# Ten gate and up chunks of layer 0 as seven block products instead of eight, and 30 adaLN units moved from the channel mixer of layer 0 into the token mixer of layer 1

## The reference, cut to what matters

```
for l in range(DEPTH):
    with_ctx = l < DEPTH - 1
    mods = jnp.split(c_act @ w_ada[l] + b_ada[l], 6, axis=-1)          # latent condition
    modc = jnp.split(cc_act @ w_ada[l] + b_ada[l], 6, axis=-1)         # context condition
    h = modulate(layernorm(x), sh1, sc1); y = token_mixers(h, hc, ...)
    x = layernorm(ALPHA * x + g1 * y)
    g, u = jnp.split(modulate(layernorm(x), sh2, sc2) @ w_gu[l], 2)    # 1024 -> 2 x 2816
    x = layernorm(ALPHA * x + g2 * ((silu(g) * u) @ w_down[l]))
```

## Time and profile before

| | us |
|---|---|
| median of 3 runs | 2298.59 (2298.22 to 2300.33) |
| the profiled execution's own time | 2300.03 |
| its span, first to last instruction | 2298.2 |
| PE busy | 2245.5 (98% of the span) |
| DVE / ACT / POOL busy | 1206.5 / 940.1 / 1108.4 |
| chain that ended last | PE 84%, DVE 8%, ACT 4% |

### The profile page before, as it was taken

One profiled execution on the slowest core, in us unless ns is written; L12 is line 12 of the kernel. 1 busy time (PEld: TensorE's weight loads), 2 busy tenths in 40 slices (PEclk: granted clock), 3 DMA queues, 4 the chain that ended last, 5 costly groups with the idle time before them and its releaser, 6 DMA issues.

```text
span 2298.2 us, 34335 instructions
## 1 busy us (share of the span) xinstructions
PE 2245.5 (98%) x12986; PEld 2054.7 (89%) x12986; DVE 1206.5 (52%) x2473; ACT 940.1 (41%) x1874; POOL 1108.4 (48%) x868
## 2 busy tenths in 40 slices
PE   7999999999999999999999999999999999999997
PEld 4899989989999999999998888888888899888887
DVE  6979766538731646654832364656637536112114
ACT  4232466437622751111112364256546547222223
POOL 1334455435534453433534563456545567545545
PEclk9999999999999999999999999999999999999999
DMA  6634300122224445443523453221223256333335
GB/s 270 218 116 133 102 19 28 57 79 82 60 65 149 154 161 183 135 154 111 167 88 118 152 170 123 69 60 38 65 87 97 83 193 189 119 96 101 110 117 186
DMA packets 122535, 270.27 MB, mean 118 GB/s; under 512 B 13972, under 2 KB 14228, under 8 KB 120984
## 3 DMA queue, kind: packets, MB, share of 16 engines
q1 hardware_dynamic: 112032, 242.28, 32.9%
q10 hardware_dynamic: 10360, 26.09, 3.5%
HBM read 254.68 MB, written 10.49 MB: 115 GB/s over the span
## 4 chain that ended last, share of the span: by engine, by line
PE 84%; DVE 8%; ACT 4%; POOL 1%; issue 1%; DMA 1%; ACTq 1%; SPq 0%; DVEq 0%
PE ps L2047 32%; PE ps L2059 13%; PE ps L2049 12%; PE ps L2476 7%; PE ps L2160 7%; PE ps L2429 3%; PE ps L2411 3%; PE ps L2392 2%; PE ps L2236 1%; POOL w_lo L610 1%; DVE pt L1741 1%; DVE max_c L1724 1%; DVE ada_unused_merge_c L1261 1%; DMA raw<-in_stream 1%; ACT p_sb L987 1%
## 5 line engine op out<-in xcount | busy, mean ns | idle before, releaser
L610 POOL TENSOR_TENSOR w_lo<-raw,w_hi 128x512 fp32r<-128x512 f32 x648 | 888.5, 1394 | 915.9 <-ACT w_hi L688 915.1
L688 ACT ACTIVATE w_hi<-raw 128x512 fp32r<-128x512 f32 x648 | 377.4, 627 | 663.7 <-PE ps L2049 215.1
L2047 PE MATMUL ps<-h_hi,w_lo 128*128 128x512 f32 (+1 forms) x832 | 304.7, 366 | 0.0
L2047 PE MATMUL ps<-h_hi,w_hi 128*128 128x512 f32 (+1 forms) x832 | 303.9, 365 | 0.0
L2047 PE MATMUL ps<-h_lo,w_hi 128*128 128x512 f32 (+1 forms) x832 | 303.9, 365 | 0.0
L622 POOL TENSOR_TENSOR p_sb<-p_sb,row_inv 128x768 f32<-128x768 f32 (+1 forms) x160 | 179.1, 1128 | 196.6 <-DVE row_inv L1734 195.2
L1851 DVE TENSOR_TENSOR ps<-silu_g,ps 128x512 f32<-128x512 f32 (+3 forms) x52 | 36.7, 706 | 355.1 <-PE ps L2047 191.1
L2047 PEld LDWEIGHTS ps<-h_hi,w_lo 128*128 128x128 f32 x832 | 156.2, 188 | 18.6 <-POOL w_lo L610 0.3
L2047 PEld LDWEIGHTS ps<-h_lo,w_hi 128*128 128x128 f32 x832 | 156.2, 188 | 18.4
L2047 PEld LDWEIGHTS ps<-h_hi,w_hi 128*128 128x128 f32 x832 | 156.2, 188 | 18.3
L2476 PE MATMUL ps<-h_hi,w_lo 128*128 128x384 f32 (+1 forms) x408 | 146.7, 360 | 1.0 <-ACT gates_a L1024 0.7
(11 more groups left out here) (248 smaller groups left out, 5345.1 us busy)
## 6 DMA issues: line engine op xcount, KB each, us to landing
raw<-in_stream SPq DMA_DIRECT2D x648, 256.0 KB, 3.0
ada_raw_gate_up<-in_w_ada SPq DMA_DIRECT2D x48, 512.0 KB, 3.5
ada_raw_tokens_a<-in_w_ada SPq DMA_DIRECT2D x16, 512.0 KB, 4.7
ada_raw_merge_c<-in_w_ada SPq DMA_DIRECT2D x16, 512.0 KB, 3.7
bias_sb<-in_bias ACTq DMA_DIRECT2D x32, 256.0 KB, 2.9
scratch<-xr ACTq DMA_DIRECT2D x16, 512.0 KB, 4.7
xr<-scratch SPq DMA_DIRECT2D x14, 512.0 KB, 5.0
first_raw<-in_w_first SPq DMA_DIRECT2D x5, 1024.0 KB, 14.4
```

Of the source, the lines that this page charges most:

```text
L610: nc.gpsimd.tensor_tensor(w_lo[:, u % 2, cols], raw[:, u % 2, cols], w_hi[:, u % 2, cols].bitcast(F32), ALU.subtract).then_inc(S("lo_made" ...
L688: nc.scalar.activation(w_hi[:, s, cols], raw[:, s, cols], ACT.Copy).then_inc(S("hi_made"), 1)
L2047: last = nc.tensor.matmul(bank(0), tile, x[:, k, 0:split], start=start, stop=stop)
```

## The change

**Seven products.** For ten chunks of layer 0 (the 6 of part 1 and the 4 wide ones of part 2) gate and up are computed together. The weights of a chunk are a 2 by 2 block matrix (gate or up by the lower or upper four channel blocks, G0, G1, U0, U1, half a unit each), and the activations are 2 by 2 too (channel half by token half). Each of the seven products (`factor` 0 to 6) takes one half-unit of weights, 4 channel blocks x 3 terms x 384 columns, 12 matmuls. Three factors are G0, G1 and U1 as they were loaded; four are sums that DVE makes in `raw` and `factor_sum` (`first_sums_of`, `last_sum_of`). On the other side three factors use `h_hi` and `h_lo`, and four use combinations `crossed`. DVE makes these once, in ten operations of 1536 columns during down part 0 (`crossing`); ACT rounds the four (`crossed_his`, in its list between the splits of units 104 and 105, the last two of down part 0), and DVE makes their rests (`crossed_rest`). Products are added up in PSUM by PE and by five DVE operations of 384 columns a chunk. ACT splits, and POOL makes the rests of, 7 half-units a chunk instead of 4. The four half-unit slots of `w_hi` and `w_lo` are taken in turn, so factor j+4 is split when factor j is done. `load_unit` of the next chunk waits for the factors that read the half, and for the chunk's fourth sum.

**adaLN.** Units 48 to 65 stay beside gate_up part 0 and down part 0. Units 66 to 95 go into layer 1: 15 into tokens_a, 15 into merge_c, with their loads in SP's list at the steps of `ADA_LOADS`. From unit 64 on only the latent condition is computed (one DVE operation a unit in place of two).

```diff
-ADA_WINDOWS = {"tokens_a": (16, 32), "merge_c": (32, 48)}
-ADA_LOADS = {"tokens_a": {2: 3, 3: 3, 4: 3, 5: 3, 6: 3, 7: 1}, "merge_c": {3: 3, 7: 2, 8: 3, 9: 2, 10: 3, 11: 3}}
-ADA_AFTER_PAIR = (4, 6, 6, 0)
-ADA_BESIDE = {("gate_up", 0): (48, 4), ("down", 0): (60, 4), ("gate_up", 1): (72, 3), ("down", 1): (81, 4),
-              ("gate_up", 2): (93, 1)}
+ADA_WINDOWS = {("tokens_a", 0): (16, 32), ("merge_c", 0): (32, 48), ("tokens_a", 1): (66, 81), ("merge_c", 1): (81, 96)}
+ADA_LOADS = {... ("tokens_a", 1): {2: 3, 3: 3, 4: 3, 5: 3, 6: 3}, ("merge_c", 1): {3: 3, 7: 2, 8: 3, 9: 2, 10: 3, 11: 2}}
+ADA_AFTER_PAIR = ((4, 6, 6, 0), (4, 6, 5, 0))
+ADA_BOTH = 64
+ADA_BESIDE = {("gate_up", 0): (48, 4), ("down", 0): (60, 2)}
+FACTOR_BANK = (0, 1, 3, 2, 0, 2, 1)
+SUMMED_FACTOR = {1: 1, 3: 2, 2: 3, 6: 4}
...
             def load_unit(u):
...
-                    if u >= 2:
+                    held = seven_of(u - 2)
+                    if held:
+                        n, up = divmod(u - 2 - held.unit, 2)
+                        wait_for(sp, factor_lo(held, SEVEN * n + ((2, 4), (3, 5))[up][half]))
+                        if not up:
+                            sp.wait_ge(S("factor_summed"), at(held, "factor_summed") + 4 * n + 4)
...
+            def seven_products(ph):                                  (ACT)
+                for j in range(last):
+                    n, i = divmod(j, SEVEN)
+                    wait_for(act, factor_done(ph, j))
+                    if i == 0:
...
+                        nc.scalar.activation(pair_p1, ps[:, bank, 0:HALF], ACT.Copy).then_inc(S("first_out"), 1)
+                    if j + 4 < last:
+                        wait_for(act, factor_done(ph, factor_held(ph, j + 4)))
+                        factor_split(ph, j + 4)
...
+                    if i == 6:
+                        act.wait_ge(S("combined"), at(ph, "combined") + 5 * n + 5)
+                        nc.scalar.activation(halves(silu_seven[:, 0, :], TOK), product(bank, TOK), ACT.Silu).then_inc(S("silu"), 1)
...
+            def crossed_his(ph):
+                act.wait_ge(S("crossed"), CROSS_STEPS)
+                for x in range(4):
+                    nc.scalar.activation(crossed_hi[x][:, :, :], crossed[x][:, :, :], ACT.Copy).then_inc(S("crossed_hi"), 1)
...
+            def down(ph):                                            (ACT)
+                        if n < KD - 2:
+                            unit_done(ph.unit + n, n % 2)
...
+                        if n == KD - 4 and ph.part == 0:
+                            crossed_his(ph)
...
             def tokens_a(ph):                                        (DVE)
...
+                else:
+                    dve.wait_ge(S("cond_loaded"), 16 * 6)
+                    ada_units(ph.kind, first, end)
                 dve.wait_ge(S("evacuated"), at(ph, "evacuated") + ph.tiles + ALLT)
...
             def merge_c(ph):                                         (DVE)
                     pair(acc[:, c, 0:w], c)
-                    if c % 2 and not ph.layer:
-                        ada_units(ph.kind, n, n + ADA_AFTER_PAIR[c // 2])
+                    if c % 2:
+                        ada_units(ph.kind, n, n + ADA_AFTER_PAIR[ph.layer][c // 2])
                     if c == 1 and ROTATED_FIRST[ph.layer] < ALLT:
                         rotate(ph, ROTATED_FIRST[ph.layer], ALLT)
...
+            def seven_products(ph):                                  (DVE)
+                for n in range(ph.chunks):
+                    last_sum_of(ph, n)
...
+                    nc.vector.tensor_tensor(pair_u2, b, pair_p1, ALU.add).then_inc(S("combined"), 1)
...
+                    if n + 1 < ph.chunks:
+                        first_sums_of(ph, n + 1)
...
+                    chunk_of_hidden(ph, n, 0, n, 0, TOK, seven_bank(n) + 2, True, silu_seven)
...
+            def seven_products(ph):                                  (PE)
+                for j in range(SEVEN * ph.chunks):
...
+                    wait_for(pe, factor_lo(ph, j))
+                    for k in range(KD // 2):
+                        for name in TERMS:
+                            last = nc.tensor.matmul(ps[:, bank, 0:HALF], half_slot(w, slot)[:, k * P:(k + 1) * P], x[:, first + k, a:a + HALF], ...)
```

More of the change, by code:

```diff
@@ L186, in last_rows, with sevenfold, factor_slot, factor_held @@
     return ph.kind == "bridge" and ph.part == 1 and ph.layer == DEPTH - 1 and g == len(ph.groups) - 1
+def sevenfold(ph):
+    return ph.kind == "gate_up" and ph.tiles == ALLT and ph.part > 0
+def factor_slot(ph, j):
+    rest = -SEVEN * ph.chunks % 4
+    return (j + sum(j >= 2 * SEVEN * (x + 1) for x in range(rest))) % 4
+def factor_held(ph, j):
+    return max(x for x in range(j) if factor_slot(ph, x) == factor_slot(ph, j))
 def ada_beside(ph):
@@ L478, in prime, with factor_of, half_slot, factor_count @@
             eng.sem_inc(S(name), PRIME)
+    def factor_of(ph, j):
+        n, i = divmod(j, SEVEN)
+        slots = raw[:, 0, 0:HALF_UNIT], raw[:, 0, HALF_UNIT:], raw[:, 1, 0:HALF_UNIT], raw[:, 1, HALF_UNIT:]
+        return (slots[0], factor_sum[:, :], slots[0], slots[2], slots[1], slots[3], factor_sum[:, :])[i]
+    def half_slot(w, q):
+        return w[:, q // 2, HALF_UNIT * (q % 2):HALF_UNIT * (q % 2 + 1)]
+    def factor_count(ph, j, names, before, early):
+        n, i = divmod(j, SEVEN)
+        few, many = names
+        if early:
+            return (few, at(ph, few) + 3 * n + i + 1) if i < 3 else (many, before + 4 * n + i - 2)
+        if i in (3, 6):
+            return many, before + 2 * n + i // 3
+        return few, at(ph, few) + 5 * n + (i + 1 if i < 3 else i)
+    def factor_done(ph, j):
+        return factor_count(ph, j, ("factor_done", "unit_done"), ph.unit, False)
+    def factor_hi(ph, j):
+        return factor_count(ph, j, ("factor_hi", "hi_made"), 2 * ph.unit, True)
+    def factor_lo(ph, j):
+        return factor_count(ph, j, ("factor_lo", "lo_made"), 2 * ph.unit, True)
+    def wait_for(eng, name_and_count):
+        name, count = name_and_count
+        eng.wait_ge(S(name), count)
+    def seven_of(u):
+        for ph in phases:
+            if sevenfold(ph) and ph.unit <= u < ph.unit + ph.units:
+                return ph
+        return None
     TERMS = ("lo_hi", "hi_lo", "hi_hi")
@@ L539, in window @@
             def window(ph, u):
-                loads = ADA_LOADS[ph.kind]
+                loads = ADA_LOADS[ph.kind, ph.layer]
                 step = u - ph.unit
@@ L550, in window @@
                     load_cond(ph.kind)
-                n = ADA_WINDOWS[ph.kind][0] + sum(count for other, count in loads.items() if other < step)
+                n = ADA_WINDOWS[ph.kind, ph.layer][0] + sum(count for other, count in loads.items() if other < step)
                 load_ada(ph.kind, n, loads[step])
@@ L556, in beside @@
                 first, count = ada_beside(ph)
-                each = 4 if ph.kind == "gate_up" and ph.part else 2
-                n, rest = divmod(u - ph.unit - 2, each)
+                n, rest = divmod(u - ph.unit - 2, 2)
                 if rest or n not in range(count):
@@ L594, in _ @@
                         load_rows(ph, u)
-                    elif ph.kind in ADA_WINDOWS and ph.layer == 0:
+                    elif (ph.kind, ph.layer) in ADA_WINDOWS:
                         window(ph, u)
@@ L1494, in tokens_a @@
             def tokens_a(ph):
+                first, end = ADA_WINDOWS[ph.kind, ph.layer]
                 if ph.layer:
@@ L1985, in several, with beside_down @@
                                         mods_v[:, ph.layer, 5, bass.ds(n, 1), c]) for a, b, c in stretches(w)])
-                if beside:
+                        if unrolled:
+                            beside_down(n)
+                nxt = after(ph)
+                steps = []
+                if sevenfold(nxt) and ph.part == 0:
+                    dve.wait_ge(S("stored"), at(ph, "stored"))
+                    dve.wait_ge(S("normed"), at(ph, "normed"))
+                    steps = crossing(ph)
+                def beside_down(n):
+                    for step in steps[2 * n:2 * n + 2]:
+                        step()
+                    if n == KD - 3 and steps:
+                        ada_biased(ADA_UNITS, ADA_BOTH, MODS_READY[1, 0])
+                        for x in range(4):
+                            crossed_rest(x)
+                    if n == KD - 2:
+                        first_sums_of(nxt, 0)
+                if sevenfold(nxt):
                     for i in range(KD // DOWN_BANKS):
```

203 lines of the change are left out of this document (176 added, 27 removed).

## The result

| | kernel before | changed kernel |
|---|---|---|
| median, 13 runs each | 2299.65 us (2297.82 to 2302.86) | 2304.08 us (2300.73 to 2307.77) |
| profiled execution: time, span | 2300.03, 2298.2 | 2303.17, 2301.4 |
| PE busy, matmuls recorded | 2245.5, 12986 | 2228.9, 12866 |
| mean granted clock | 0.997 | 0.992 |

A forecast was written before the change was run, and what follows sets the result against it. PE, busy 98% of the span, was taken to bound the kernel. Terms -20.8 - 1.1 + 9.3 + 5.5 + 4.2 + 0.5 + 3.4 = +1.0 us gave 2299.6 us; range for eight in ten 2281 to 2313, own 2293 to 2307.

The forecast's parts named there:

- Ten chunks: Gate_up chunks of layer 0: 84 matmuls instead of 96 at 0.1733 us each, saving 20.8 us.
- Rival C: Seven products: 84 matmuls but a slower pitch, at 0.190 us a saving of 5 us, time 2315; chance 0.02.
- Wait in down part 1: Down part 1, layer 0: the adaLN units that leave take a PE wait with them, saving 1.1 us.
- tokens_a: Layer 1: unit 173's load stands behind adaLN loads waiting for DVE; PE waits 9.3 us, bounds 8.0 to 11.1.
- merge_c: Layer 1: unit 184's load stands behind an adaLN load waiting for DVE; PE waits 5.5 us, bounds 4 and 7.
- down part 0: Layer 0: ACT's roundings wait for DVE's list, delaying unit 105's split; PE waits 4.2 us, bounds 0 to 8.
- Inside the chunks: Ten gate_up chunks: no engine full, no steady wait, 0.5 us for starts and ends, bounds 0 to 3.
- rival B: Ten gate_up chunks: the closed loop is the bound, at 16.3 us a chunk giving 2317; chance 0.22.
- my loop: In each chunk, DVE's fourth sum through loads, landing, sums and silu to the next: 12.5 to 16.3 us, taken as 14.2.
- Clock: Behind the three waits: PE's granted clock falls, 1.7 us once and 0.85 twice, 3.4 us; bounds 0 to 5.1.
- Meetings of VectorE and POOL: Down part 0: DVE operations with two SBUF inputs meeting POOL's w_lo cost 0.95 us each, eight adding 7.6.
- Rival A: All three wait places: the waits do not come, only 0 to 6 us come back, 2281; chance 0.20.

The follow-up runs named there:

- e2: Changed kernel with merge_c's adaLN loads in layer 1 later and other numbers of adaLN operations behind the pairs: 2300.41 us, ratio 1.0005.
- e4: Changed kernel with adaLN loads of tokens_a and merge_c in layer 1 later and the four roundings behind unit 105's split: 2286.31 us, ratio 0.995.
- e3: Changed kernel with ACT's four roundings of the crossed activations behind unit 105's split, not ahead of it: 2299.44 us, ratio 1.0002.
- e7: Changed kernel with 40 unused matmuls on PE between units 172 and 173 of tokens_a in layer 1: 2303.51 us, ratio 1.0012.
- e9: Changed kernel with one more DVE operation, result unused, ahead of the fourth sum in each of the ten chunks: 2304.05 us, ratio 1.002.
- e5: Changed kernel with 12 adaLN units in layer 0's late gate_up chunks, 12 in tokens_a, 6 in merge_c, roundings behind unit 105's split: 2278.68 us, ratio 0.9904.

## Why the prediction was right, step by step

The time came out 4.5 us over the forecast, inside its own range of 2293 to 2307, and the mechanism was the forecast one: a whole saving, given back in three waits. 1.1 of the 4.5 us are the kernel before, whose median moved from 2298.59 to 2299.65. That the sum came so close is in part luck: single terms were off by up to 2 us, in both directions, and what I had for merge_c was only half of its mechanism. By its terms (predicted, measured in the profiled executions):

- **Ten chunks**, -20.8: -20.9. The pitch read from the bridge holds. Rival C is out. (Its price was miscounted: 840 matmuls at 0.190 us are 159.6, a saving of 6.8 us of 166.4 and not 5.)
- **Wait in down part 1**, -1.1: -1.9. I took only the stretch behind 1090 us; the stage as a whole was 1.85 us longer than its 288 matmuls at the pitch.
- **tokens_a**, +9.3: 10.1. Step by step: rope_g was to end at 1399.1, which is 1379.2 once the 19.9 us gained ahead of it are taken off; it ended at 1378.75. SP was to issue unit 173 at 1383.7 and did at 1383.09. The landing was to take 4.3 us and took 5.7. Here lies the difference; I took the value of down part 1, where the DMA share from 1110 to 1120 us is 0.64; here it is 0.95. The page of the kernel before already had 4.7 us for the adaLN loads of tokens_a in layer 0 against 3.5 beside gate_up, a sign that I didn't use.
- **merge_c**, +5.5: 7.5 (6.72 and 0.82), over my upper bound of 7. The chain to unit 184 was the forecast one. PE came to it 6.8 us earlier than in the kernel before, so its load was to go out at 1482.3 and did at 1482.72; the landing took 4.4 us and not 3.9, and these with 0.1 more behind the landing make the wait about 1.2 us longer than forecast. The last unit of the phase, for which I had seen "within 0.5", was late by 0.82. e2 and e4 showed what the step lacked: I followed one load and not DVE's total in the phase, so another order of the loads looked like a cure.
- **down part 0**, +4.2: 2.7. The list ended at 980.92 (predicted 981.3), which was the uncertain part. The four roundings took 5.62 us and not 6.3, since they overlap at their ends, and PE got its first half-unit at 988.79 where I had 989.7 to 991.4. A mis-sized term, with the right chain; e3 confirms its place. In two other executions of the same code the clock fell behind this wait, and the stage cost 4.4 and 4.5.
- **Inside the chunks**, +0.5: 0. PE has no wait in the ten chunks, but rival B, to which I gave 0.22, was nearer than my 14.2 us says: in the last two wide chunks w_lo of the second factor was ready 0.27 and 0.13 us before PE took it, in the others 0.7 to 3.0. Though the adaLN loads are gone from these stages, the half-units of part 1 landed in 3.6 us in the middle (2.5 to 5.2), where my loop had 3.0.
- **Clock**, +3.4: 4.4 us of slow matmuls (2.9 and 1.5), none in down part 0 in this execution. The wait of 2.44 us left the granted clock at 1.00, that of 6.72 took it to 0.50. The even chance that I gave the shorter waits was a fair reading: behind the wait in down part 0 the clock fell in two of seven executions. The Trainium skill (TensorE: Matmul & The Clock Gate, "What's actually happening") has idleness bring the 1.2 GHz level; e7 agrees, with PE at work and the clock at 1.00. But its price is no constant: e7 puts it at 1.5 net in tokens_a.
- **Meetings of VectorE and POOL.** The Trainium skill (SBUF — State Buffer, "SBUF: two separate sides") has them exclude each other for a whole operation. e9 shows what can follow for a sum of costs: in three of its ten chunks the operation put ahead of the meeting was paid by a shorter meeting (1.55 to 0.98 us in the third); in the other seven the sum ended 1.4 to 2.1 us later. So a meeting can't be charged, or credited, by one chunk.

By stretches, waits and slow clock together, the sum is -20.9 - 1.9 + 2.7 + 13.2 + 9.4 + 0.6 = +3.1. Rival A, that the waits do not come, was wrong as a forecast of this kernel and right as a description of what it could be: e5, 2278.68, against its 2281.

What stays open: the 1.3 us between the medians' difference (4.4) and the profiled executions' (3.1) is within the interval, and the clock behind the wait in down part 0, which cost 1.7 us in two executions and nothing in this one, may be a part of it; e3's 4.6 against 2.7 is open in the same way. And whether some other order of merge_c's 15 loads would remove its wait was not tried beyond e2's.
